# First mixer layer's r projection as seven block products placed behind q and k, in a two-layer GLA / chunked-attention trunk

## Chip, core and metric

The kernel runs on one core of one Trainium2 chip. The metric is device time in microseconds (us) of one execution; lower is better. Everything is float32 to the outside. TensorE works on fp32r operands, and each float32 operand is split into a high and a low part, so that one product of two float32 tiles is three matmuls (hi x hi, hi x lo, lo x hi).

## What is computed

Two layers on 512 tokens of width 1024. Layer 0 is gated linear attention (GLA), then a SwiGLU feed-forward; layer 1 is chunked softmax attention, then a feed-forward; each is followed by a layer norm with a residual. The change lies in the GLA mixer alone:

```python
q, k, v, r, g_low = split(x @ w_in, [512, 1024, 2048, 3072])    # x: 512 x 1024
log_a = log_sigmoid(g_low @ w_gate_up + b_gate) / 16
cum = cumsum(log_a)                       # within chunks
q_dec = q * exp(cum);  k_inv = k * exp(-cum);  k_end = k * exp(total - cum)
a = causal(q_dec @ k_inv^T);  o = a @ v + q_dec @ state
state = state * exp(total) + k_end^T @ v
y = silu(r) * layernorm(o) * norm_g
out = y @ w_out
```

r is x (512 x 1024) times a 1024 x 1024 weight. It is used only in the last step, as the gate of the normalised o.

## The kernel before

The program is written by hand for five engines, each with its own instruction list; semaphores order them. Weights come as "slabs" of 128 x 1024 floats, two to a DMA of 1 MB (a pair), issued by SP into one of two raw buffers (`raw`, slot = pair number modulo 2; the feed-forward's down projection has two more). A raw slot is free when both slabs of its pair are split. ACT copies a slab to `w_hi` (`split_hi`, line 638), then POOL (line 1179) or VectorE (DVE, line 1330) subtracts to get `w_lo`. `w_hi` and `w_lo` are rings of four slabs: `split_hi(n)` waits until TensorE (PE) is done with slab n-4 (`slab_done`), and PE waits for the low part (`lo_done`) of the slab it begins. ACT, DVE, POOL and SP each work in program order, so a wait holds everything behind it on that engine.

The GLA stage has the slabs in this order: v (8), r (8), q and k (8, alternating by head), then the output projection (8, `GLA_OUT`). PE's order:

- `token_major(0, GLA_V, ...)`: v, 24 matmuls of 128x512 to a slab. Each of the two halves of v's columns fills four PSUM banks, which ACT copies out (line 893).
- 16 matmuls for the gate's low-rank input (lines 2283, 2284), then r by `token_major(1, GLA_R, ...)`, 24 matmuls to a slab, with four matmuls of the gate (`gate_up`) after r's first slab. ACT applies Silu straight from the banks (line 932) and POOL multiplies by `norm_g` (line 1255).
- q and k, 24 matmuls to a slab. In the meantime DVE runs the cumulative sums (line 1795) and ACT the exponentials (lines 915 to 920), and DVE scales q and k out of the banks (lines 1814 to 1821).
- The recurrence over four tiles of 128 tokens: `turn_ke` (transposes of k_end, line 2317), `gla_scores` (line 2324), `updates` (line 2331), `intra` (line 2338), `inter` (line 2346), `turn_y` (line 2140). Around it ACT copies o out (`copy_o`) and normalises it (`normalise_o`, line 951), DVE masks scores (line 1833), updates the state (lines 1847, 1849), takes the statistics (`stats_o`, lines 1872, 1875), the shift (line 1882) and the gate product (`gate_o`, line 1859), and POOL takes the root (lines 1263, 1264) between the two.
- The output projection of GLA, the feed-forward, and so on.

The feed-forward's down projection already works by seven half-size block products (the Winograd form of Strassen's scheme). Its sums of weight blocks are made in DRAM by DMAs that POOL issues (`block_sum`, lines 1207 and 1209; every second one adds into its destination), each waiting for the one before. The tables that it uses are the ones that the change uses too:

```python
INTO = ("x", "z", "y", "x", "y", "x", "w")
SOURCES = (("down", 0), ("down", 2), ("sums", 0), ("sums", 1), ("down", 3), ("sums", 2), ("sums", 3))
SUM_STEPS = ((0, "down", 0), (0, "down", 1), (1, "sums", 0), (1, "down", 3),
             (2, "down", 1), (2, "down", 3), (3, "sums", 1), (3, "down", 2))
SUM_READY = {2: 2, 3: 4, 5: 6, 6: 8}
```

`SUM_READY` says how many of the eight DMAs must have landed before product p's weights may be loaded. In the down projection pair q (of 20) takes slot q modulo 4, whatever the parity of the pairs before.

## Time and profile before

| | us |
|---|---|
| median of 3 runs | 1132.55 (1132.28 to 1132.69) |
| the profiled execution, whole | 1132.14 |
| its span in the profile | 1130.40 |
| TensorE busy in the span | 1120.2 (99%) |
| DVE / ACT / POOL busy | 784.6 / 569.8 / 325.6 |

The span is the time from the first to the last instruction in the profile; 1.74 us of the profiled execution lie outside it. Times in the trace count from the span's start. PE's matmuls are pipelined: the interval from one start to the next is its pace, and the shown duration is longer. A weight load overlaps the matmul before it. Idle time of an engine other than the one that sets the end costs nothing by itself.

### The profile page before, as it was taken

Reading aid. Unit: us, or ns where it says so; the run is one execution under the profiler, and the core shown is the slowest. Engines: PE = TensorE matmul, PEld = TensorE weight load, DVE = VectorE, ACT = ScalarE, POOL = GpSimd, SP = SyncE. Lnnn points to the kernel's source line nnn. Section 1 sums busy time; section 2 is a strip of 40 time slices with the busy share of each in tenths; the row PEclk is TensorE's granted clock in tenths of the full one; section 3 lists DMA queues with packets and bytes.
Section 4 is the critical chain, followed back from the end, with each engine's and each line's share of the span. In section 5 each row is a group of like instructions: output and inputs, shape, how many; then the busy total and the mean of one; then the engine's idle time right before and its main releaser. Section 6 shows DMA issues by size and latency. Waiting matters only on the chain.

```text
span 1130.4 us, 18412 instructions
## 1 busy us (share of the span) xinstructions
PE 1120.2 (99%) x6828; PEld 994.7 (88%) x6828; DVE 784.6 (69%) x1263; ACT 569.8 (50%) x926; POOL 325.6 (29%) x215
## 2 busy tenths in 40 slices
PE   9999999999999999999999999999999999999997
PEld 7888888989999999888887787778989999998886
DVE  5070163798888885998604676766878888868987
ACT  4345144244555556555515565772445555556553
POOL 1538525142222112000445343551412222230001
PEclk9999999999999999999999999999999999999999
DMA  6433314076897764654332212132159879827551
GB/s 227 167 150 112 112 38 149 13 271 164 273 279 211 245 182 175 234 197 170 108 112 75 95 47 94 48 150 75 38 191 279 237 248 280 214 74 298 189 193 75
DMA packets 34459, 183.35 MB, mean 162 GB/s; under 512 B 3152, under 2 KB 7376, under 8 KB 20704
## 3 DMA queue, kind: packets, MB, share of 16 engines
q1 hardware_dynamic: 19472, 122.27, 30.1%
q0 software_dynamic: 8448, 46.14, 15.8%
...
## 4 chain that ended last, share of the span: by engine, by line
PE 96%; DVE 1%; issue 1%; DMA 1%; ACT 0%; POOL 0%; SPq 0%; DVEq 0%; POOLq 0%; ACTq 0%
PE bank L2057 29%; PE bank L2059 29%; PE bank L2058 29%; PE bank L2509 2%; PE bank L2493 2%; PE bank L2140 1%; PE bank L2088 1%; PE bank L2530 1%; PE bank L2529 1%; DMA s_raw<-stream 1%; PE bank L2338 1%; DVE s_w_lo L1330 1%; PE bank L2331 0%; PE bank L2346 0%; PE bank L2324 0%
## 5 line engine op out<-in xcount | busy, mean ns | idle before, releaser
L2057 PE MATMUL bank<-s_t_hi,s_w_hi 128*128 128x256 f32 (+1 forms) x832 | 264.4, 318 | 0.0
L2058 PE MATMUL bank<-s_t_lo,s_w_hi 128*128 128x256 f32 (+1 forms) x832 | 262.8, 316 | 0.0
L2059 PE MATMUL bank<-s_t_hi,s_w_lo 128*128 128x256 f32 (+1 forms) x832 | 262.8, 316 | 0.0
L1179 POOL TENSOR_TENSOR s_w_lo<-s_raw,s_w_hi 128x1024 fp32r<-128x1024 f32 x64 | 160.1, 2512 | 180.3 <-ACT s_w_hi L638 180.3
L638 ACT ACTIVATE s_w_hi<-s_raw 128x1024 fp32r<-128x1024 f32 x107 | 111.3, 1057 | 114.6 <-PE bank L2059 90.5
L2059 PEld LDWEIGHTS bank<-s_t_hi,s_w_lo 128*128 128x128 f32 x832 | 158.6, 191 | 10.2
L2057 PEld LDWEIGHTS bank<-s_t_hi,s_w_hi 128*128 128x128 f32 x832 | 158.7, 191 | 9.7 <-issue 0.2
L2058 PEld LDWEIGHTS bank<-s_t_lo,s_w_hi 128*128 128x128 f32 x832 | 158.7, 191 | 9.4
L1216 POOL TENSOR_TENSOR s_w_lo<-s_raw,s_w_hi 128x512 fp32r<-128x512 f32 x36 | 67.2, 1866 | 274.3 <-ACT s_w_hi L768 274.3
L2057 PE MATMUL bank<-s_t_hi,s_w_s_hi 128*128 128x256 f32 x432 | 122.4, 283 | 0.0
L2059 PE MATMUL bank<-s_t_hi,s_w_s_lo 128*128 128x256 f32 x432 | 122.2, 283 | 0.0
L2058 PE MATMUL bank<-s_t_lo,s_w_s_hi 128*128 128x256 f32 x432 | 122.2, 283 | 0.0
L2057 PE MATMUL bank<-s_w_hi,s_t_hi 128*128 128x512 f32 x264 | 104.2, 395 | 0.0
L2059 PE MATMUL bank<-s_w_hi,s_t_lo 128*128 128x512 f32 x264 | 102.9, 390 | 0.0
L2058 PE MATMUL bank<-s_w_lo,s_t_hi 128*128 128x512 f32 x264 | 102.8, 389 | 0.0
L2057 PEld LDWEIGHTS bank<-s_t_hi,s_w_s_hi 128*128 128x128 f32 x432 | 82.9, 192 | 0.1
L2058 PEld LDWEIGHTS bank<-s_t_lo,s_w_s_hi 128*128 128x128 f32 x432 | 82.9, 192 | 0.0
L2059 PEld LDWEIGHTS bank<-s_t_hi,s_w_s_lo 128*128 128x128 f32 x432 | 82.9, 192 | 0.0
L1187 POOL TENSOR_SCALAR s_var_eps<-s_variance 128x1 f32<-128x1 f32 x15 | 4.9, 324 | 244.5 <-ACT s_squared L672 244.5
L1330 DVE TENSOR_TENSOR s_w_lo<-s_raw,s_w_hi 128x1024 fp32r<-128x1024 f32 x40 | 48.9, 1222 | 28.5 <-ACT s_w_hi L638 14.1
L2059 PEld LDWEIGHTS bank<-s_w_hi,s_t_lo 128*128 128x128 f32 x264 | 49.6, 188 | 10.5
L2057 PEld LDWEIGHTS bank<-s_w_hi,s_t_hi 128*128 128x128 f32 x264 | 49.6, 188 | 10.1 <-DVE s_t_lo L1336 0.2
...
## 6 DMA issues: line engine op xcount, KB each, us to landing
s_raw<-stream SPq DMA_DIRECT2D x75, 1024.0 KB, 4.8
sums<-down POOLq DMA_DIRECT2D x12, 2816.0 KB, 20.9
s_more_raw<-sums SPq DMA_DIRECT2D x12, 1024.0 KB, 4.9
sums<-sums POOLq DMA_DIRECT2D x4, 2816.0 KB, 12.9
s_raw<-down SPq DMA_DIRECT2D x8, 1024.0 KB, 4.9
s_ln_gb<-ln_gb ACTq DMA_DIRECT2D x4, 1024.0 KB, 7.0
s_more_raw<-down SPq DMA_DIRECT2D x4, 1024.0 KB, 7.5
s_raw<-sums SPq DMA_DIRECT2D x4, 1024.0 KB, 4.9
```

The source lines that it names most:

```text
L638: nc.scalar.activation(w_parts(n, cols)[0], raw_pair(SLOTS[pair])[:, n % 2, cols], ACT.Copy).then_inc(hi_done, new)
L1179: nc.gpsimd.tensor_tensor(lo, raw_pair(SLOTS[place // 2])[:, n % 2, cols], hi.bitcast(F32), ALU.subtract).then_inc(lo_done, new)
L1216: nc.gpsimd.tensor_tensor(w_lo[:, up_at, HALF:], raw[:, slot, 1, HALF:], w_hi[:, up_at, HALF:].bitcast(F32), ALU.subtract).then_inc(lo_don ...
L1330: nc.vector.tensor_tensor(lo, raw_pair(SLOTS[place // 2])[:, n % 2, cols], hi.bitcast(F32), ALU.subtract).then_inc(lo_done, new)
L2057: nc.tensor.matmul(out, l_hi, r_hi, start=start, stop=False, skip_group_check=skip)
L2058: nc.tensor.matmul(out, l_hi, r_lo, start=False, stop=False, skip_group_check=skip)
L2059: return nc.tensor.matmul(out, l_lo, r_hi, start=False, stop=stop, skip_group_check=skip)
L2088: last = nc.tensor.matmul(bank[bank_of(0, t)][:, :], x, w, start=(k == 0 and low_x + low_w == 0), stop=False)
L2140: last = nc.tensor.transpose(bank[banks[t][half]][:, k * P:(k + 1) * P], src[:, t, (4 * half + k) * P:(4 * half + k + 1) * P], ident[:, :])
L2338: last = nc.tensor.matmul(bank[GLA_O_BANKS[t][hd // 2]][:, (hd % 2) * GLA_DV:(hd % 2 + 1) * GLA_DV], g_am[:, t % 2, hd * P:(hd + 1) * P], ...
L2493: last = nc.tensor.matmul(bank[2 + hd][:, score_columns(t)], qk[q][rows, toks], qk[k][rows, keys], start=(i == 0), stop=(i == 2))
L2509: last = nc.tensor.transpose(bank[4 + hd][:, at:at + P], r_p[:, s % 4, j * P:(j + 1) * P], ident[:, :])
```

## The change

r moves behind q and k, and is computed by seven products of half size instead of eight slabs. A product is 512 x 512 of weights (two slabs of 12 matmuls each) with 256 tokens and 4 blocks of 128 of the inner dimension, so 24 matmuls of 128x512. Four products use sums of weight blocks (`r_sums` in DRAM, made by eight DMAs of POOL of 1 MB each), four use sums of blocks of x (`r_ops`, made by DVE, laid where `h` and `ln_gb` will be loaded, and in one case in `g_rg`). ACT copies the products out of the banks to `g_rg` (`r_copy`), DVE adds the second part (`r_add`), then come Silu and `norm_g` as before, now from SBUF. The loads of `h` and `ln_gb` are issued only after the sixth product. The low parts of the product weights are DVE's for 10 of 14 slabs. The first tile's `turn_ke` and `gla_scores` go ahead of the seventh product. q and k of the first two heads are copied out by ACT (`copy_qk`) and scaled from SBUF. Some semaphores are merged, which changes no order by itself. The core of the diff:

```diff
-GLA_R = GLA_V + KD
-GLA_QK = GLA_R + KD
-GLA_OUT = GLA_QK + 2 * GLA_HEADS
+GLA_QK = GLA_V + KD
+GLA_R = GLA_QK + 2 * GLA_HEADS
+GLA_OUT = GLA_R + 2 * 7
+R_SUM_BYTES = KD // 2 * HALF
...
+        R_BANKS = {"x": (0, 1), "y": (4, 5), "z": (6, 7), "w": (2, 3)}
+        R_QUARTERS = ((0, 0), (1, 0), (0, 1), (1, 1), (2, 1), (3, 1), (2, 0), (3, 0))
...
+                if GLA_R <= n < GLA_OUT:
+                    p = (n - GLA_R) // 2
+                    if p in SUM_READY:
+                        sp.wait_ge(r_blocks, 16 * SUM_READY[p])
+                    array, which = SOURCES[p]
+                    sp.dma_start(raw_pair(slot).rearrange("p a c -> p (a c)"), a["r_" + array][which]).then_inc(raw_full[slot], 16)
+                    continue
...
+            def r_op_highs():
+                for i in range(3):
+                    act.wait_ge(r_op_sum, i + 1)
+                    nc.scalar.activation(r_ops[i]["hi"][:, :, :], r_ops[i]["sum"][:, :, :], ACT.Copy).then_inc(r_op_hi, 1)
...
+            r_split(0, 5)
+            r_done(0)
+            act.wait_ge(qk_scaled, 6)
+            r_copy("x", 0)
+            r_copy("x", 1)
...
+            r_split(11, 14)
+            for n in range(GLA_OUT, GLA_OUT + 2):
+                split_hi(n)
+            r_silu(2)
+            r_silu(3)
+            r_done(5)
+            act.dma_start(h[:, :, :], a["x"].rearrange("(t p) d -> p t d", p=P)).then_inc(h_full, 16)
+            load_gb(0)
+            act.wait_ge(r_op_lo, 4)
+            r_copy("x", 6)
+            r_copy("x", 7)
...
+            ke_tile_out(0)
+            r_silu(4)
+            r_silu(5)
+            split_hi(GLA_OUT + 2)
+            r_silu(6)
+            r_silu(7)
...
+            def r_block_sum(step):
+                to, array, which = SUM_STEPS[step]
+                if step:
+                    pool.wait_ge(r_blocks, 16 * step)
+                if step % 2:
+                    nc.gpsimd.dma_start(a["r_sums"][to], a["r_" + array][which], accum_op=ALU.add,
+                                        max_dma_last_dim=R_SUM_BYTES).then_inc(r_blocks, 16)
+                else:
+                    nc.gpsimd.dma_start(a["r_sums"][to], a["r_" + array][which], max_dma_last_dim=R_SUM_BYTES).then_inc(r_blocks, 16)
+
             for n in range(GLA_V, GLA_R):
                 split_lo(n + RING)
+                if n % 2 == 1:
+                    r_block_sum(n // 2)
...
+            scale_r(0)
+            scale_r(1)
+            pool.wait_ge(lo_done, GLA_OUT)
+            scale_r(2)
+            scale_r(3)
+            split_lo(GLA_OUT)
+            for quarter in range(4, 8):
+                scale_r(quarter)
+            split_lo(GLA_OUT + 1)
+            root_o(0)
+            split_lo(GLA_OUT + 2)
+            root_o(1)
...
+            r1, r2, r4 = (r_ops[i]["sum"][:, :, :] for i in range(3))
+            nc.vector.tensor_tensor(r1, x_half(0, LATE_TOKS), x_half(1, LATE_TOKS), ALU.subtract).then_inc(r_op_sum, 1)
+            dve.wait_ge(r_op_sum, 1)
+            nc.vector.tensor_tensor(r2, r1, x_half(0, EARLY_TOKS), ALU.subtract).then_inc(r_op_sum, 1)
...
+            dve.wait_ge(lo_done, GLA_R + RING)
+            r_low(4, 7)
+            dve.wait_ge(slab_done, GLA_R + 4)
+            dve.wait_ge(r_copied, 2)
+            r_add(0, None, "z", ALU.add)
+            r_add(1, None, "z", ALU.add)
+            r_low(7, 10)
+            dve.wait_ge(r_op_hi, 4)
+            r_op_low(0, g_rg[:, 2:4, 0:HALF].rearrange("p t (k c) -> p t k c", k=2))
+            r_low(10, 14)
+            dve.wait_ge(slab_done, GLA_R + 10)
+            dve.wait_ge(r_copied, 6)
+            r_add(2, "y", None, ALU.subtract)
+            r_add(3, "y", None, ALU.subtract)
...
-            token_major(1, GLA_R, lambda half, t: 4 - 4 * half + t, r_free, beside=gate_up)
...
+            for p in range(PRODUCTS):
+                if p == 0:
+                    pe.wait_ge(abs_done, GLA_HEADS)
+                    pe.wait_ge(min_done, GLA_HEADS)
+                if p == 1:
+                    pe.wait_ge(qk_scaled, 3 * GLA_HEADS)
+                if 2 <= p <= 5:
+                    pe.wait_ge(r_op_lo, p - 1)
+                if 3 <= p <= 5:
+                    pe.wait_ge(r_copied, 2 * (p - 2))
+                if p == PRODUCTS - 1:
+                    pe.wait_ge(consts, 7)
+                    pe.wait_ge(r_merged, 4)
+                    turn_ke(0)
+                    gla_scores(0)
+                op_hi_, op_lo_ = r_operand(p)
+                for j in range(KD // 2):
+                    n = GLA_R + 2 * p + j // 2
+                    if j % 2 == 0:
+                        pe.wait_ge(lo_done, place_of(n) + 1)
+                    for i in range(2):
+                        toks = slice(i * P, (i + 1) * P)
+                        last = three(bank[R_BANKS[INTO[p]][i]][:, :], op_hi_[:, j, toks], op_lo_[:, j, toks],
+                                     *w_parts(n, slice(j % 2 * HALF, (j % 2 + 1) * HALF)),
+                                     INTO[p] not in INTO[:p] and j == 0, j == KD // 2 - 1, True)
+                    if j % 2:
+                        last.then_inc(slab_done, 1)
```

On POOL the stretch from the first weight split to the recurrence's first two roots stands so before (`s_w_lo` is a slab's low part, `s_g_rg` is r times `norm_g`, `s_var_eps_o` and `s_rstd_o` are the root):

```order
L1179 TENSOR_TENSOR s_w_lo<-s_raw,s_w_hi 128x1024 x12
L1255 TENSOR_TENSOR s_g_rg<-s_g_rg,s_norm_g 128x512 x2
L1179 TENSOR_TENSOR s_w_lo<-s_raw,s_w_hi 128x1024
L1255 TENSOR_TENSOR s_g_rg<-s_g_rg,s_norm_g 128x512 x2
L1179 TENSOR_TENSOR s_w_lo<-s_raw,s_w_hi 128x1024 x3
L1255 TENSOR_TENSOR s_g_rg<-s_g_rg,s_norm_g 128x512 x4
L1179 TENSOR_TENSOR s_w_lo<-s_raw,s_w_hi 128x1024 x8
L1263 TENSOR_SCALAR s_var_eps_o<-s_mv_o 128x4
L1264 TENSOR_TENSOR s_rstd_o<-s_var_eps_o,s_minus_half 128x4
```

and so of the change, from the seventh of the eight sums on:

```order
L1320 DMA r_sums<-r_sums 512x512
L1247 TENSOR_TENSOR s_w_lo<-s_raw,s_w_hi 128x1024 x2
L1317 DMA r_sums<-r_down 512x512
L1332 TENSOR_TENSOR s_g_rg<-s_g_rg,s_norm_g 128x512 x4
L1247 TENSOR_TENSOR s_w_lo<-s_raw,s_w_hi 128x1024
L1332 TENSOR_TENSOR s_g_rg<-s_g_rg,s_norm_g 128x512 x4
L1247 TENSOR_TENSOR s_w_lo<-s_raw,s_w_hi 128x1024
L1336 TENSOR_SCALAR s_var_eps_o<-s_mv_o 128x4
L1337 TENSOR_TENSOR s_rstd_o<-s_var_eps_o,s_minus_half 128x4
L1247 TENSOR_TENSOR s_w_lo<-s_raw,s_w_hi 128x1024
```

The sums stand between pairs of weight splits, and all eight products by `norm_g` now stand behind the last sum, with two splits of the output projection between them and the first root, and one more split between the first root and the second.

On ACT, around the sixth and seventh product and the recurrence's first turn, the change has this (`s_g_kt` is the copy of the turned k_end, L966 is Silu, L960 the copy of a product out of its bank):

```order
L655 ACTIVATE s_w_hi<-s_raw 128x1024 x5
L966 ACTIVATE s_g_rg<-s_g_rg 128x512 x2
L994 DMA s_h<-x 128x4x1024
L670 DMA s_ln_gb<-ln_gb 128x2048
L960 ACTIVATE s_g_rg<-bank 128x512 x2
L1004 ACTIVATE s_g_kt<-bank 128x512
L966 ACTIVATE s_g_rg<-s_g_rg 128x512 x2
L655 ACTIVATE s_w_hi<-s_raw 128x1024
L966 ACTIVATE s_g_rg<-s_g_rg 128x512 x2
L1004 ACTIVATE s_g_kt<-bank 128x512
```

Before, ACT had this there:

```order
L932 ACTIVATE s_g_rg<-bank 128x512 x4
L638 ACTIVATE s_w_hi<-s_raw 128x1024 x7
L942 ACTIVATE s_g_kt<-bank 128x512
L638 ACTIVATE s_w_hi<-s_raw 128x1024
L942 ACTIVATE s_g_kt<-bank 128x512
```

The copy of the first turned tile, for which PE's `updates(0)` waits, stands behind five weight splits, two Silus, two DMA issues and two bank copies; before, only weight splits stood ahead of it.

## Rows read from the trace of the kernel before

**Rows 1.** The page: busy time of each engine, and the clock granted to TensorE.

```profile
PE 1120.2 (99%) x6828; PEld 994.7 (88%) x6828; DVE 784.6 (69%) x1263; ACT 569.8 (50%) x926; POOL 325.6 (29%) x215
...
PEclk9999999999999999999999999999999999999999
```

**Rows 2.** Waits of PE, longest first: total us, times, longest.

```profile
PE bank L2277 <- DVE s_g_am L1735: 1.4, 1, 1.4
PE bank L2509 <- DVE s_pt_lo L1953: 0.8, 2, 0.5
PE bank L2088 <- ACT s_w_hi L876: 0.3, 1, 0.3
```

**Rows 3.** Timeline of PE, v: start, us, what (first and last of 120).

```profile
23.01 0.39 PE L2057 MATMUL bank<-s_w_hi,s_t_hi 128*128 128x512 f32 x1
...
49.98 0.39 PE L2059 MATMUL bank<-s_w_hi,s_t_lo 128*128 128x512 f32 x1
50.21 0.39 PE L2283 MATMUL bank<-s_t_hi,s_wg 128*128 128x512 f32 x1
```

**Rows 4.** Timeline of PE, the recurrence.

```profile
141.79 0.60 PE L2317 MATMUL bank<-s_ident,s_g_ke 128*128 128x128 f32 x4
142.22 1.06 PE L2324 MATMUL bank<-s_g_q,s_g_ki 128*128 128x128 f32 x8
143.16 1.97 PE L2331 MATMUL bank<-s_g_v,s_g_kt 128*128 128x256 f32 x8
...
160.61 1.04 PE L2140 MATMUL bank<-s_ident,s_g_on 128*128 128x128 f32 x8
```

**Rows 5.** The page's DMA issues: KB of each, median us to landing.

```profile
s_raw<-stream SPq DMA_DIRECT2D x75, 1024.0 KB, 4.8
sums<-down POOLq DMA_DIRECT2D x12, 2816.0 KB, 20.9
...
sums<-sums POOLq DMA_DIRECT2D x4, 2816.0 KB, 12.9
...
bias_rows<-rel_bias ACTq DMA_DIRECT2D x1, 3072.0 KB, 12.3
```

**Rows 6.** Timeline of POOL: four sum DMAs of the down projection.

```profile
242.87 0.90 POOL L1209 DMA_DIRECT2D sums<-down  x1
...
268.16 1.07 POOL L1207 DMA_DIRECT2D sums<-down  x1
...
290.54 0.67 POOL L1209 DMA_DIRECT2D sums<-sums  x1 [4.11 <-DMA sums<-down]
...
307.83 1.02 POOL L1207 DMA_DIRECT2D sums<-down  x1 [1.24 <-DMA sums<-sums]
```

**Rows 7.** Timeline of DVE while POOL splits weights, with one add just before.

```profile
230.04 0.69 DVE L1588 TENSOR_TENSOR s_t_sum<-s_t_sum,s_t_lo 128x512 f32<-128x512 f32 x1
...
231.37 2.60 DVE L1588 TENSOR_TENSOR s_t_sum<-s_t_sum,s_t_lo 128x512 f32<-128x512 f32 x1
```

**Rows 8.** Timeline of POOL, splits: beside those DVE adds, and in v.

```profile
231.01 2.41 POOL L1179 TENSOR_TENSOR s_w_lo<-s_raw,s_w_hi 128x1024 fp32r<-128x1024 f32 x1 [13.87 <-ACT s_w_hi L638]
...
25.46 9.52 POOL L1179 TENSOR_TENSOR s_w_lo<-s_raw,s_w_hi 128x1024 fp32r<-128x1024 f32 x4 [22.19 <-ACT s_w_hi L638]
```

**Rows 9.** Timeline of ACT: splits of slabs, copies of banks, Silu.

```profile
24.24 3.19 ACT L638 ACTIVATE s_w_hi<-s_raw 128x1024 fp32r<-128x1024 f32 x3
...
90.52 2.07 ACT L932 ACTIVATE s_g_rg<-bank 128x512 f32<-128x512 f32 x4
```

**Rows 10.** Timeline of DVE: a slab's low part, the first statistics, last mask.

```profile
19.26 1.22 DVE L1751 TENSOR_TENSOR s_w_lo<-s_raw,s_w_hi 128x1024 fp32r<-128x1024 f32 x1
...
149.34 1.41 DVE L1872 BATCH_NORM_STATS2 s_bn_o<-s_g_on 128x6 f32<-128x256 f32 x4 [2.12 <-ACT s_g_on L961]
...
159.65 0.73 DVE L1833 COPY_PREDICATED s_g_am<-s_causal,bank 128x512 f32<-128x512 int32 x1
```

**Rows 11.** Timeline of POOL: products by norm_g, and the first root.

```profile
91.64 2.55 POOL L1255 TENSOR_TENSOR s_g_rg<-s_g_rg,s_norm_g 128x512 f32<-128x512 f32 x2
...
151.25 0.24 POOL L1263 TENSOR_SCALAR s_var_eps_o<-s_mv_o 128x4 f32<-128x4 f32 x1 [4.85 <-DVE s_mv_o L1875]
```

**Rows 12.** Timeline of SP: first loads of the down projection, loads behind it.

```profile
417.55 10.47 SPq L600 DMA_DIRECT2D s_raw<-down  x2
...
529.16 5.12 SPq L592 DMA_DIRECT2D s_raw<-stream  x2
```

**Rows 13.** Timelines: ACT's splits of those loads, and DVE behind the last.

```profile
433.92 1.05 ACT L638 ACTIVATE s_w_hi<-s_raw 128x1024 fp32r<-128x1024 f32 x1
...
537.46 1.99 ACT L638 ACTIVATE s_early<-s_raw 128x1024 fp32r<-128x1024 f32 x2
...
543.13 1.28 DVE L1336 TENSOR_TENSOR s_t_lo<-bank,s_t_hi 128x512 fp32r<-128x512 f32 x2
```

More of the change, by code:

```diff
@@ L180, in build_program @@
         t_lo = sb("t_lo", [P, KD, SEQ], F32R)
+        h_at = place[0]
         h = sb("h", [P, TILES, D_MODEL])
@@ L312, in build_program @@
         wg_raw = get("wg_raw", [P, KD, GLA_RANK])
+        qk_raw = sb_at("qk_raw", [P, 2, 2, SEQ], F32, rg_at)
+        r_ops = [halves_at(f"r_op{i}", [P, KD // 2, SEQ // 2], at_, at_ + 4 * KB)
+                 for i, at_ in enumerate((h_at, h_at + 8 * KB, gb_at))]
         get, _ = carve(on_at, region_end)
@@ L653, in load_gb, with token_major @@
                 act.dma_start(ln_gb[:, :, :], a["ln_gb"][n].partition_broadcast(P)).then_inc(gb_full, 16)
-            def token_major(which, n0, bank_of, copy_out):
+            def token_major(which, n0, bank_of, copy_out, between=None):
                 for half in range(2):
+                    if half == 1 and between is not None:
+                        between()
                     for k in range(KD // 2):
@@ L911, in _, with copy_qk @@
             nc.scalar.activation(g_e[:, :, :], g_e[:, :, :], ACT.Ln, bias=1.0).then_inc(log_done, 1)
-            for n in range(GLA_R, GLA_R + EARLY_R):
+            def copy_qk(hd, is_k):
+                act.wait_ge(slab_done, GLA_QK + 2 * hd + is_k + 1)
+                nc.scalar.activation(qk_raw[:, hd, is_k, :], bank[4 + 2 * hd + is_k][:, :], ACT.Copy).then_inc(qk_copied, 1)
+            for n in range(GLA_QK, GLA_QK + EARLY_QK):
                 split_hi(n + RING)
-            act.wait_ge(centred_cum, 1)
+            for hd in range(2):
+                for is_k in range(2):
+                    copy_qk(hd, is_k)
@@ L935, in _, with r_split, r_done, r_copy @@
-            for n in range(GLA_QK, GLA_OUT - 1):
-                split_hi(n + RING)
+            def r_split(first, end):
+                for slab in range(first, end):
+                    split_hi(GLA_R + slab)
+            def r_done(p):
+                act.wait_ge(slab_done, GLA_R + 2 * p + 2)
+            def r_copy(b, quarter):
+                t, half = R_QUARTERS[quarter]
+                nc.scalar.activation(g_rg[:, t, half * HALF:(half + 1) * HALF], bank[R_BANKS[b][t % 2]][:, :],
+                                     ACT.Copy).then_inc(r_copied, 1)
@@ new lines, in r_silu @@
+            def r_silu(quarter):
+                t, half = R_QUARTERS[quarter]
+                act.wait_ge(r_merged, quarter + 1)
+                nc.scalar.activation(g_rg[:, t, half * HALF:(half + 1) * HALF], g_rg[:, t, half * HALF:(half + 1) * HALF],
+                                     ACT.Silu).then_inc(tok_out[1], 1)
+            r_split(0, 5)
[3 more added lines that the diff above has]
+            r_copy("x", 1)
+            r_split(5, 8)
@@ new lines, in _ @@
+            r_silu(0)
+            r_silu(1)
+            r_split(8, 9)
+            r_done(2)
+            act.wait_ge(r_op_sum, 4)
+            nc.scalar.activation(r_ops[0]["hi"][:, :, :], g_rg[:, 2:4, 0:HALF].rearrange("p t (k c) -> p t k c", k=2),
+                                 ACT.Copy).then_inc(r_op_hi, 1)
+            r_copy("y", 4)
+            r_copy("y", 5)
+            r_split(9, 11)
+            r_done(3)
+            r_copy("x", 2)
+            r_copy("x", 3)
+            r_split(11, 14)
@@ new lines, in r_low, with r_add @@
+            def r_low(first, end):
+                for slab in range(first, end):
+                    split_low(GLA_R + slab)
+            def r_add(quarter, first, second, op):
+                t, half = R_QUARTERS[quarter]
+                out = g_rg[:, t, half * HALF:(half + 1) * HALF]
+                first, second = (out if b is None else bank[R_BANKS[b][t % 2]][:, :] for b in (first, second))
+                nc.vector.tensor_tensor(out, first, second, op).then_inc(r_merged, 1)
+            dve.wait_ge(lo_done, GLA_R + RING)
@@ L1834, in mask_scores @@
                                           bank[4][:, :]).then_inc(sc_masked, 1)
+            dve.wait_ge(am_zeroed, 3)
+            dve.wait_ge(consts, 7)
+            mask_scores(0)
+            dve.wait_ge(slab_done, GLA_R + 14)
+            r_add(6, None, "w", ALU.add)
+            r_add(7, None, "w", ALU.add)
             def update_state(t):
@@ L2353, in turn_y @@
                 turn(GLA_YT, t, g_on, GLA_Y_BANKS)
-            pe.wait_ge(consts, 7)
             pe.wait_ge(tok_out[0], 2 * TILES)
-            pe.wait_ge(qk_scaled, 3 * GLA_HEADS - 1)
-            turn_ke(0)
-            gla_scores(0, range(GLA_HEADS - 1))
-            pe.wait_ge(qk_scaled, 3 * GLA_HEADS)
-            gla_scores(0, (GLA_HEADS - 1,))
-            pe.wait_ge(tok_out[1], 2 * TILES)
             for t in range(TILES):
@@ L2376, in _ @@
                 pe.wait_ge(sc_masked, t + 1)
+                if t == 0:
+                    pe.wait_ge(r_merged, 2 * TILES)
                 if t >= 2:
```

176 lines of the change are left out of this document (91 added, 85 removed).

## The prediction

> **What bounds the kernel now.** I read the page first. TensorE (PE) is busy for 99% of the span and its clock stands at the full level (2.4 GHz) in all 40 slices [rows 1]. A busy PE alone proves little, since its durations overlap, so I went to PE's waits: over the whole run they add up to some 3 us, and the longest after the start is 0.5 us [rows 2]. In the stretch that the change touches, 6 to 190 us, PE waits for nobody after v's first slabs. So time falls by the matmuls taken from PE, less the waits that the new order makes. The third view is PE's timeline. Through v, 120 matmuls of 128x512 start from 23.01 to 50.21 us, where the next line begins [rows 3]: 27.20 / 120 = 0.2267 us each. The recurrence runs at the same kind of pace from 141.79 us on, with nothing between its lines [rows 4].
>
> **Removed from PE.** r was 8 slabs of 24 such matmuls, 192, or 43.5 us. It becomes 7 products of 24, 168, or 38.1 us, of the same shape. 24 x 0.2267 = **5.44 us** less. Nothing is added on PE: `turn_ke(0)` and `gla_scores(0)`, 1.37 us from 141.79 to 143.16 [rows 4], only stand ahead of the seventh product. What is left is whether everybody can keep up. I walked the new order by hand from 25 to 160 us, each instruction at the interval that the rows show for its kind and each wait at the later of its two sides. New times below are from this walk: q starts at 53.8, the products at 98.3, the recurrence's `updates(0)` at 137.7, and the output projection is reached 5.4 to 5.7 us earlier than before.
>
> **The weight sums.** Eight DMAs of 1 MB by POOL, each waiting for the one before, stand between POOL's splits from 31 us on, so a late sum holds the splits behind it. Before has no DMA of 1 MB of this kind. The nearest are the down projection's, of 2.75 times the bytes: 20.9 us, or 12.9 for the copy of a sum [rows 5]. One by one, the copy issued at 242.87 and the add at 268.16 show what POOL's next issue waits for: it goes out at 290.54, some 22 us behind the add, and the copy of 290.54 has landed by 307.83 [rows 6]. By bytes alone a copy of 1 MB is 12.9 / 2.75 = 4.7 and an add 20.9 / 2.75 = 7.6 us; that is the lower bound. The upper one is no gain from size, 13 and 21 us, because both kinds have 512 rows (here of 2 KB instead of 5.5). The bias copy, 3 MB in rows of 1.5 KB, lands in 12.3 us [rows 5], so short rows alone do not make a copy slow. I take 6 and 9 us, near the lower end with a little for a fixed part. In the walk the last sum, behind the split of slab 19, is issued at 102 and lands at 111, and the load that needs it goes out at 119. Nothing waits up to 9 and 12 us, beyond 0.3. At 9 and 13 PE loses 1.3 us, at 10 and 14 it loses 7.7, at 13 and 21 some 46.
>
> **POOL and DVE together.** A DVE add of 128x512 with all operands in SBUF took 0.69 us just before POOL's split, and 2.60 us when it began 0.36 us into that split [rows 7, 8]: POOL's 2.41 us end at 233.42, and 0.6 later the add ends. One waits for the other. The change puts three adds and three low parts of x between POOL's splits of slabs 4 to 7, which ran without a gap before, 9.52 us for four [rows 8]. Taking turns, slab 7's low part comes at 43.1 us instead of 35, and PE wants it at 44.8. It holds, with 1.6 us left. The same turns can push the low part of the gate's rank-16 input behind a split: in the walk it ends 0.4 us before `gate_up` at 59.3, and in the worst phase it is late by 1.2. I take 0 to 1.2, near 0.2.
>
> **Splits and loads for the products.** A slab now lasts PE 12 x 0.2267 = 2.72 us. With a ring of four, three slabs (8.2 us) lie between a freed place and the need for it. ACT's split takes 1.0 us and a bank copy 0.5 [rows 9], DVE's low part 1.2 [rows 10]. A pair's load, 4.8 us [rows 5], has six slabs (16.3 us) less both splits. With the bank copies, adds and Silus in between, the least margin of the walk is 3.2 us, ahead of the fifth product. `turn_ke(0)` wants the adds of quarters 2 and 3, with 1.7 us left, and `updates(0)` wants `ke_tile_out(0)`, which ACT has behind its splits and the two DMA issues, with 2.0 left. `intra(0)` wants the last two adds, with 1.5 left. These edits cost nothing while these margins last; each us beyond them is a us on PE.
>
> **POOL before the first root.** The eight products by `norm_g`, 1.27 us each (2.55 for two) [rows 11], now end in a row of six with two splits that begins at 132.7 us, when ACT has done Silu 2, and ends at 145.0. The first root is wanted when the statistics are done, at 145.6 (before, 9.5 us behind `turn_ke(0)`: 151.25 [rows 11]). It is free 0.7 us early. What queues behind the root is the shift, the second mask, `gate_o(0)`, the second statistics, and in the end the last mask, for which `turn_y(0)` waits. Before, that mask was done at 160.38 [rows 10] and `turn_y(0)` began at 160.61 [rows 4], so that chain has only some 0.3 us to give. If the statistics (149.34, 1.41 us, one input in SBUF [rows 10]) wait for POOL's last split as the adds in rows 7 do, it all moves by 1.2 us and PE loses 0.8; if not, 0. I take 0, for only the adds with two inputs have been seen waiting.
>
> The Trainium skill, SBUF — State Buffer, section "Who interferes with whom", has this as a lock that VectorE takes with two SBUF inputs and that it and GpSimd hold for a whole instruction. By that rule the statistics, with one input, go free and the sum keeps its 5.44 us; read from the add's row alone without telling the inputs apart, it would be 4.7.
>
> **The parity of pairs.** r has 6 slabs more, so every later pair has the other raw slot, but the down projection begins at slot 0 all the same. Its first load then follows directly on the pair that is freed last: its two first loads went out at 417.55 and by 427.69 us [rows 12] (10.47 in all, with 0.33 for the issue), and now both go at the second time. The split of the first came at 433.92 [rows 13]; 427.7 + 4.8 = 432.5, in time by 1.4 us, in both layers. Behind layer 0's down projection the load of 529.16 likewise moves to the time of the next, 534.0 (529.16 + 5.12 less the issue) [rows 12], and lands near 538.8, where ACT's split stood at 537.46 [rows 13]: 1.3 us late on ACT, ahead of the transposed tiles, for which DVE had its step only at 543.13 [rows 13]. I take 0, and up to 1.3 as the bound.
>
> **Sum.** 1130.40 - 5.44 + 0.3 for small waits = 1125.3 us of span; with 1.74 us outside it 1127.0. The profiled execution was 0.41 us under the median of the runs, so **1127.4 us**.
>
> **The rivals.** A difference under 0.2% (2.3 us) is about what a measurement here cannot tell from none.
> - The case above, with 0 to 1.2 us of waits: 1127.1 to 1128.3. For it speaks that each margin came out positive. Chance 0.65.
> - The recurrence's first turn is late, as POOL reaches the root behind its eight products (a split beside DVE's work has taken more than 2.4 us). Each us past 0.7 at the root is nearly one on PE. With 2 us: 1129.1. Against it: DVE reads PSUM in most of that stretch. 0.10.
> - The sums land late. This is the one that can end slower: from 10 and 14 us for copy and add the 5.4 us are gone (1134.8 with 7.7 lost), and every further us per pair costs more. At 9 and 13: 1128.4. Against it stands the bias copy's row. For it stand equal row counts and loads beside them. 0.14, of it 0.03 faster, 0.05 same, 0.06 slower.
> - The other raw slot holds up a transition: 1 to 3 us, so 1129.1. 0.07, of it 0.02 same.
> - The change does not do what it says: the products' matmuls run slower than v's, as they change operands between `t_hi`, `r_ops` and two token tiles, or a wait that I did not see. v too changes its stationary tile at each three matmuls and keeps 0.2267. 1132 to 1136. 0.04.
>
> **How the numbers follow.** Faster by over 0.2% (under 1130.3): 0.65 + 0.07 of the second case (the rest of it, 0.03, falls within 0.2%) + 0.03 + 0.05 = 0.80. Same: 0.03 + 0.05 + 0.02 + 0.02 = 0.12. Slower: 0.06 + 0.02 = 0.08. The range begins at 1126.7, for 5.44 us and the 0.3 us by which the recurrence could start with less of a gap, and reaches to 1131.5, which leaves some 0.12 above. The likeliest case alone has 1126.7 to 1128.3.
>
> **What would show it.** Right: PE without a wait over 0.5 us between 50 and 165 us; the products from about 98.3 to 137.7; the output projection 5.4 us earlier; the sum DMAs landing in 5 to 10 us, the last by 112. Wrong: PE waiting for `s_w_lo` in the second product (late sums), for `s_g_am` or `s_g_rg` in the recurrence (late root or adds), for `s_low_rows` near 59 (turns of POOL and DVE), or for `s_w_lo` at 436 or 1013 (parity).

## The result, and the profile after

| | before | changed |
|---|---|---|
| median of 9 runs each, us | 1132.38 (1131.97 to 1132.69) | 1135.66 (1133.33 to 1137.72) |
| the profiled execution, whole / span | 1132.14 / 1130.40 | 1133.33 / 1131.3 |
| mean granted clock | 0.999 in the profiled execution, 0.998 to 0.999 in the later batches | 0.993 to 0.999 over the nine runs |

The changed kernel is slower by 3.3 us: ratio 1.0029, 95% interval 1.0019 to 1.0039. The prediction, 1127.4 us in a range of 1126.7 to 1131.5, is missed, and on the other side of no change. The profiled execution is the fastest of the nine: its span is only 0.9 us longer than before's. So the profile shows a part of the loss, and the median has more.

The page of the changed kernel, answering to [rows 1]:

```profile
PE 1115.3 (99%) x6804; PEld 990.2 (88%) x6804; DVE 840.9 (74%) x1290; ACT 587.7 (52%) x948; POOL 326.1 (29%) x219
```

PE has 24 matmuls and 4.9 us of busy time less, and the products run at v's pace: from the start of the third at 111.39 us, 66 matmuls take 14.96 us, 0.2267 each. PE's waits in the changed kernel, total us, times, longest, beside [rows 2]:

```profile
PE bank L2288 <- DVE s_g_am L1978: 3.8, 1, 3.8
PE bank L2205 <- DVE s_g_ki L1936: 2.5, 1, 2.5
PE bank L2425 <- DVE s_g_am L1824: 1.4, 1, 1.4
PE bank L2682 <- DVE s_pt_lo L2101: 0.8, 2, 0.5
```

The two upper waits are new. L2205 is the first matmul of the second product, which waits for q and k to be scaled; L2288 is `turn_y(0)`, which waits for the last mask. 1130.4 - 5.44 + 2.49 + 3.77 = 1131.2, which is the profiled span of 1131.3. So in this execution these terms account for the whole span.

**The first wait.** DVE in the changed kernel, the scalings of heads 0 and 1, and then the first that reads a bank; below it POOL in the same stretch:

```profile
89.93 0.69 DVE L1930 SCALAR_TENSOR_TENSOR s_g_q<-s_qk_raw,s_g_q 128x512 f32<-128x512 f32 x1 [3.05 <-ACT s_g_ke L949]
90.53 0.55 DVE L1934 TENSOR_TENSOR s_g_ke<-s_qk_raw,s_g_ke 128x384 f32<-128x384 f32 x1
91.00 2.90 DVE L1936 TENSOR_TENSOR s_g_ki<-s_qk_raw,s_g_ki 128x512 f32<-128x512 f32 x1
93.83 2.88 DVE L1930 SCALAR_TENSOR_TENSOR s_g_q<-s_qk_raw,s_g_q 128x512 f32<-128x512 f32 x1
96.63 3.00 DVE L1934 TENSOR_TENSOR s_g_ke<-s_qk_raw,s_g_ke 128x384 f32<-128x384 f32 x1
99.55 2.88 DVE L1936 TENSOR_TENSOR s_g_ki<-s_qk_raw,s_g_ki 128x512 f32<-128x512 f32 x1
102.36 0.68 DVE L1930 SCALAR_TENSOR_TENSOR s_g_q<-bank,s_g_q 128x512 f32<-128x512 f32 x1
```

```profile
90.92 5.23 POOL L1247 TENSOR_TENSOR s_w_lo<-s_raw,s_w_hi 128x1024 fp32r<-128x1024 f32 x2 [6.54 <-ACT s_w_hi L655]
...
96.78 5.11 POOL L1247 TENSOR_TENSOR s_w_lo<-s_raw,s_w_hi 128x1024 fp32r<-128x1024 f32 x2
```

Before POOL's first split an operation takes 0.55 to 0.69 us; beside the four splits it takes 2.9 to 3.0, so the two alternate, one DVE operation to one split. Four times some 2.3 us of extra time put the end of the last scaling at 105.76, and PE starts at 105.81. The same line, L1930, is fast again at 102.36, when the splits have ended and it reads a bank (`a` below tells these two apart).

The chain ahead of the scalings was late as well. The four cumulative sums (line 1908) took 13.13 us beside four splits, where they had taken 10.97 beside three (line 1795). The exponentials and the first scaling stand behind them. Up to 2.2 of the 2.5 us may therefore be their share; no run takes it apart.

**The second wait.** DVE behind the two roots, and POOL there:

```profile
146.08 1.41 DVE L2021 BATCH_NORM_STATS2 s_bn_o<-s_g_on 128x6 f32<-128x256 f32 x4 [2.10 <-ACT s_g_on L1030]
...
149.47 2.23 DVE L2031 SCALAR_TENSOR_TENSOR s_shift_o<-s_mv_o,s_rstd_o 128x4 f32<-128x4 f32 x1
151.63 0.73 DVE L1978 COPY_PREDICATED s_g_am<-s_causal,bank 128x512 f32<-128x512 int32 x1
...
158.37 2.21 DVE L2031 SCALAR_TENSOR_TENSOR s_shift_o<-s_mv_o,s_rstd_o 128x4 f32<-128x4 f32 x1
160.51 0.71 DVE L1978 COPY_PREDICATED s_g_am<-s_causal,bank 128x512 f32<-128x512 int32 x1
```

```profile
144.94 2.35 POOL L1247 TENSOR_TENSOR s_w_lo<-s_raw,s_w_hi 128x1024 fp32r<-128x1024 f32 x1
...
147.99 0.23 POOL L1336 TENSOR_SCALAR s_var_eps_o<-s_mv_o 128x4 f32<-128x4 f32 x1 [0.70 <-DVE s_mv_o L2024]
148.31 1.05 POOL L1337 TENSOR_TENSOR s_rstd_o<-s_var_eps_o,s_minus_half 128x4 f32<-128x4 f32 x1
149.34 2.34 POOL L1247 TENSOR_TENSOR s_w_lo<-s_raw,s_w_hi 128x1024 fp32r<-128x1024 f32 x1
```

The shift has 4 elements to a partition, and takes 2.2 us, because POOL began a split 0.13 us ahead of it. POOL was in time at the root (it sat idle for 0.70 us before it). The statistics at 146.08, with one input in SBUF, began within the split of 144.94 and took 1.41 us, as before. The shift, twice, delays the mask behind it, and the second one ends PE's wait.

The Trainium skill, SBUF — State Buffer, section "Who interferes with whom", says this of both places: an instruction of DVE with two SBUF inputs and one of POOL that reads SBUF hold a shared port for their whole length, and the later one blocks. The rows agree in who waits and for how long, down to an instruction of 128x4; the port itself is in no row.

### The profile page after: what moved, and what is told of

It is laid out like the page before. It is cut to its first block, busy times and chain, and to the rows that moved or that the text cites. A ratio compares the mean times of both kernels' runs of the same rounds, so it can differ in the third digit from the quotient of the medians.

```text
span 1131.3 us, 18450 instructions
## 1 busy us (share of the span) xinstructions
PE 1115.3 (99%) x6804; PEld 990.2 (88%) x6804; DVE 840.9 (74%) x1290; ACT 587.7 (52%) x948; POOL 326.1 (29%) x219
## 4 chain that ended last, share of the span: by engine, by line
PE 91%; DVE 4%; issue 2%; ACT 1%; DMA 1%; POOL 0%; DVEq 0%; POOLq 0%; SPq 0%; ACTq 0%
PE bank L2205 27%; PE bank L2207 27%; PE bank L2206 27%; PE bank L2682 2%; PE bank L2666 2%; PE bank L2236 1%; PE bank L2288 1%; DVE s_w_lo L1419 1%; PE bank L2703 1%; PE bank L2702 1%; DMA s_more_raw<-down 1%; DVE s_g_ki L1936 1%; DVE s_g_q L1930 0%; PE bank L2425 0%; DVE s_g_ke L1934 0%
## 5 line engine op out<-in xcount | busy, mean ns | idle before, releaser
L2205 PE MATMUL bank<-s_t_hi,s_w_hi 128*128 128x256 f32 (+1 forms) x832 | 264.4, 318 | 0.0
L1247 POOL TENSOR_TENSOR s_w_lo<-s_raw,s_w_hi 128x1024 fp32r<-128x1024 f32 x60 | 154.0, 2587 | 146.2 <-ACT s_w_hi L655 146.1
L655 ACT ACTIVATE s_w_hi<-s_raw 128x1024 fp32r<-128x1024 f32 x113 | 117.6, 1058 | 96.3 <-PE bank L2207 79.0
L2205 PEld LDWEIGHTS bank<-s_t_hi,s_w_hi 128*128 128x128 f32 x832 | 158.7, 191 | 9.7 <-issue 0.2
L2205 PE MATMUL bank<-s_t_hi,s_w_s_hi 128*128 128x256 f32 x432 | 122.4, 283 | 0.0
L2205 PE MATMUL bank<-s_w_hi,s_t_hi 128*128 128x512 f32 x224 | 89.0, 397 | 2.5 <-DVE s_g_ki L1936 2.5
L1419 DVE TENSOR_TENSOR s_w_lo<-s_raw,s_w_hi 128x1024 fp32r<-128x1024 f32 x50 | 61.7, 1234 | 37.8 <-ACT s_w_hi L655 23.3
L2207 PE MATMUL bank<-s_w_hi,s_t_lo 128*128 128x512 f32 x224 | 87.4, 390 | 0.0
L2206 PE MATMUL bank<-s_w_lo,s_t_hi 128*128 128x512 f32 x224 | 87.2, 389 | 0.0
L2205 PEld LDWEIGHTS bank<-s_t_hi,s_w_s_hi 128*128 128x128 f32 x432 | 82.9, 192 | 0.1
L823 ACT ACTIVATE s_prod<-bank 128x256 f32<-128x256 f32 x36 | 13.9, 385 | 85.9 <-PE bank L2207 85.9
L655 ACT ACTIVATE s_w_hi<-s_more_raw 128x1024 fp32r<-128x1024 f32 (+1 forms) x38 | 38.6, 1034 | 32.7 <-PE bank L2207 28.5
```

The lines of the kernel that those rows point to most:

```text
L655: nc.scalar.activation(w_parts(n, cols)[0], raw_pair(SLOTS[pair])[:, n % 2, cols], ACT.Copy).then_inc(hi_done, new)
L823: nc.scalar.activation(parts_of(j)[3], bank[banks["a"][j]][:, EARLY_TOKS], ACT.Silu).then_inc(gated[f], 1)
L1247: nc.gpsimd.tensor_tensor(lo, raw_pair(SLOTS[place // 2])[:, n % 2, cols], hi.bitcast(F32), ALU.subtract).then_inc(lo_done, new)
L1419: nc.vector.tensor_tensor(lo, raw_pair(SLOTS[place // 2])[:, n % 2, cols], hi.bitcast(F32), ALU.subtract).then_inc(lo_done, new)
L2205: nc.tensor.matmul(out, l_hi, r_hi, start=start, stop=False, skip_group_check=skip)
L2206: nc.tensor.matmul(out, l_hi, r_lo, start=False, stop=False, skip_group_check=skip)
```

## The experiments

Ten kernels follow; `d` and `i` leave out a factor of the shift, `e` the sums. "The mask wait" below is PE's wait ahead of `turn_y(0)`, 3.8 us in the changed kernel. Times are medians; before stood at 1132.17 to 1132.32 in the same batches.

| label | median us (runs) | ratio, 95% | profiled span |
|---|---|---|---|
| a_wait_scaled | 1133.66 (11) | 1.0014 (1.0004 to 1.0023) | 1130.8 |
| b_wait_shift | 1131.03 (11) | 0.9987 (0.9978 to 0.9996) | 1129.3 |
| ab_both_waits | 1127.60 (5) | 0.9963 (0.9949 to 0.9977) | 1125.6 |
| c_before_splits_behind_roots | 1137.64 (5) | 1.0048 (1.0034 to 1.0062) | 1135.7 |
| d_one_input_shift | 1134.01 (10) | 1.0014 (1.0004 to 1.0023) | 1132.9 |
| e_no_sums | 1126.70 (4) | 0.9951 (0.9936 to 0.9966) | 1124.7 |
| f_adds_ahead | 1126.83 (5) | 0.9955 (0.9941 to 0.9968) | 1125.1 |
| g_before_one_split | 1134.21 (10) | 1.0018 (1.0008 to 1.0027) | 1131.9 |
| i_reduce_shift | 1127.80 (6) | 0.9964 (0.9951 to 0.9976) | 1125.7 |
| j_filled_wait | 1136.67 (5) | 1.0038 (1.0024 to 1.0052) | 1134.9 |

### The first wait alone

```diff
             for n in range(GLA_V, GLA_R):
+                if n + RING == GLA_R:
+                    pool.wait_ge(qk_scaled, 6)
                 split_lo(n + RING)
```

> Edit: in the changed kernel POOL waits for the six scalings of heads 0 and 1 before it splits the products' first slab. Theory (POOL and DVE take turns on SBUF: each all-SBUF scaling waits for one POOL split): those scalings take 0.55 to 0.7 us each, all twelve end near 99.5 us in place of 105.8, and PE's wait of 2.49 us ahead of the second product is gone; the wait of 3.8 us ahead of turn_y(0) stays. Span 1128.5 to 1129.2 where the clock is 0.999, median of runs 1129.5 to 1133, since one stall of PE is left that may still bring lower granted clocks. Rival (the scalings are late because their inputs, the exponentials, are late): exps are 1.6 us later than before, so the wait ahead of the second product stays above 1.5 us and the time is unchanged at about 1135. Rival (the late weight sums matter): POOL's delayed splits put the last two sums 3 us later, and PE then waits for a low part in the products, no gain.

The first wait is gone from PE's list and the second stands, 3.7 us. So the holds of the scalings caused it, and neither rival (late exponentials alone, late sums) stands. The scalings that read a bank are not held, though they too run beside splits (0.55 to 0.68 us each, here one of them):

```profile
94.22 0.55 DVE L1936 TENSOR_TENSOR s_g_ke<-bank,s_g_ke 128x384 f32<-128x384 f32 x1
```

```profile
93.79 4.76 POOL L1247 TENSOR_TENSOR s_w_lo<-s_raw,s_w_hi 128x1024 fp32r<-128x1024 f32 x2 [10.19 <-DVE s_g_ki L1938]
```

But the span, expected at 1128.5 to 1129.2 for a clock of 0.999, is 1130.8, no run has that clock (0.995 to 0.997; spans 1130.6 to 1133.0), and the median of 1133.66 lies 0.7 above its range. The profile of this run shows a part of the reason. PE behind `turn_y(0)`'s wait, and the granted clock of stretches there (columns: stretch, its length, PE's busy time and instructions, clock, DMA share, GB/s):

```profile
159.43 1.12 PE L2290 MATMUL bank<-s_ident,s_g_on 128*128 128x128 f32 x8 [3.75 <-DVE s_g_am L1980]
160.36 3.58 PE L2518 MATMUL bank<-s_g_v,s_g_am 128*128 128x256 f32 x8
...
165.32 0.58 PE L2207 MATMUL bank<-s_w_hi,s_t_hi 128*128 128x512 f32 x1
```

```profile
160.00:161.00 1.00, 1.00 (x7) 0.68 0.55 164
161.00:162.00 1.00, 1.00 (x3) 0.50 0.99 418
162.00:163.00 1.00, 1.00 (x4) 0.50 0.91 385
163.00:164.00 1.00, 1.00 (x5) 0.61 0.01 0
164.00:165.00 1.00, 1.00 (x6) 1.00 0.00 0
```

The clock falls to the level of 1.2 GHz just behind the wait; the missing shares of these rows add up to 1.7 us. The eight matmuls of `intra(3)` take 3.58 us, and 1.89 at 2.4 GHz. From `turn_y(0)` to the output projection it is 165.32 - 159.43 = 5.89 us, and 165.47 - 161.28 = 4.19 in the profiled execution of the change, where the clock stayed up after a wait as long. So this stall cost its own length and 1.7 us more, and the span is accounted for: 1130.4 - 5.44 + 3.75 + 1.7 + 0.4 (a wait ahead of `turn_ke(0)`) = 1130.8. The slower of the eleven runs, up to 1133.0, have up to 2.2 us more that no profile shows.

### The second wait alone

```diff
             root_o(0)
+            pool.wait_ge(shift_done, 1)
             split_lo(GLA_OUT + 2)
             root_o(1)
+            pool.wait_ge(shift_done, 2)
             split_lo(GLA_OUT + 3)
```

> Edit: in the changed kernel POOL waits for the first shift before it splits GLA_OUT+2, and for the second before GLA_OUT+3. Theory (the 128x4 shift of DVE with two SBUF inputs waits for the whole split that POOL begins just before it): both shifts take 0.16 us, PE's wait of 3.77 us ahead of turn_y(0) is gone or under 0.3; the wait of 2.5 us ahead of the second product stays. Span 1127.4 to 1128.0 at a clock of 0.999; median of runs 1128.5 to 1132. Rival (the recurrence is late because POOL reaches the root late, behind its eight products by norm_g): the wait stays above 2 us, time about 1135.

The mask wait is gone and the first one stays at 2.5 us; the kernel is now slightly faster than before. Its eleven runs fall into two groups: three with spans of 1127.7 to 1127.9 at a clock of 0.999, and eight with 1129.1 to 1130.0 at 0.996 to 0.998. The profile is of the second group. PE behind the wait of 2.48 us, and the clock there:

```profile
106.35 0.80 PE L2207 MATMUL bank<-s_w_hi,s_t_hi 128*128 128x512 f32 x1 [2.48 <-DVE s_g_ki L1938]
...
107.80 0.63 PE L2207 MATMUL bank<-s_w_hi,s_t_hi 128*128 128x512 f32 x1
108.23 0.63 PE L2208 MATMUL bank<-s_w_lo,s_t_hi 128*128 128x512 f32 x1
...
109.99 0.39 PE L2207 MATMUL bank<-s_w_hi,s_t_hi 128*128 128x512 f32 x1
110.22 0.40 PE L2208 MATMUL bank<-s_w_lo,s_t_hi 128*128 128x512 f32 x1
```

```profile
107.00:108.00 1.00, 1.00 (x4) 0.50 0.93 154
108.00:109.00 1.00, 1.00 (x4) 0.50 1.14 209
109.00:110.00 1.00, 1.00 (x5) 0.75 1.11 205
110.00:111.00 1.00, 1.00 (x6) 1.00 1.12 207
```

The pace is 0.43 us to a matmul until about 109.5, and then 0.23 again. The distance of the two groups, 1.6 us between 1127.7 and 1129.3, is what this costs. The median, 1131.03, lies in the range given for it; the range for the span, given for a clock of 0.999, held for the three runs that had that clock.

### Both

> Both edits together. Theory: PE has no wait above 0.5 us between 50 and 165 us; span 1125.0 to 1125.6, whole 1126.8 to 1127.5 in every run, with a granted clock of 0.999 as in the kernel before, if it is PE's stalls that lower the clock in most runs of the changed kernel. Rival for the clock (something else in the change lowers it, as the products' order or the DMAs' load): runs still show 0.993 to 0.997 and the median stands 2 to 3 us above the fastest run.

1127.60 us. DVE's scalings take 0.55 to 0.69 us each and the shift 0.16:

```profile
91.17 0.68 DVE L1940 TENSOR_TENSOR s_g_ki<-s_qk_raw,s_g_ki 128x512 f32<-128x512 f32 x1
...
147.73 0.16 DVE L2035 SCALAR_TENSOR_TENSOR s_shift_o<-s_mv_o,s_rstd_o 128x4 f32<-128x4 f32 x1
```

```profile
...
PE bank L2240 <- ACT s_w_hi L895: 0.7, 1, 0.7
PE bank L2471 <- DVE s_g_rg L1958: 0.7, 1, 0.7
```

The theory's 0.5 us was missed by little: one new wait of 0.7 us is left between 50 and 165 us, ahead of `turn_ke(0)` (L2471; L2240 lies in v's first slabs). POOL's wait for the scalings has a part in it: it moves the last sum's issue from 103.75 to 106.0 us. The clock is 0.998 to 0.999 in every run, as before. The span, 1125.6, is 4.8 us under before's; the expected whole time held in two of five runs, the next two were within 0.15 us, and one had 1129.50, 1.6 us of span above its neighbours at a clock of 0.998, unexplained. The clocks of 0.993 to 0.997 are gone with the two waits, so the rival "something else lowers the clock" falls.

### One part of the change in the kernel before

`c` puts POOL's splits of `GLA_OUT+2` and `+3` behind the first and second root of the kernel before, and changes nothing else; `g` moves only the latter.

```diff
-            for n in range(GLA_QK, GLA_OUT):
+            for n in range(GLA_QK, GLA_OUT - 2):
                 split_lo(n + RING)
             for t in range(TILES):
...
+                if t < 2:
+                    split_lo(GLA_OUT + 2 + t)
```

> Edit in the kernel before: POOL's splits of GLA_OUT+2 and GLA_OUT+3 stand behind the first and the second root, as in the change; nothing else. Theory: the shifts take 2.2 us in place of 0.16, both in one chain, and PE waits 3.6 to 4.1 us ahead of turn_y(0); span 1134.0 to 1134.5 at 0.999, and if a stall of PE there brings lower clocks, a median of 1136 to 1139 with clocks of 0.993 to 0.997. Rival (the stall needs the change's other parts, as the later root): under 1 us, 1132 to 1133.5.

> Edit in the kernel before: only POOL's split of GLA_OUT+3 stands behind the second root. Theory: the second shift alone takes 2.2 us, PE waits 1.7 to 1.9 us ahead of turn_y(0): span 1132.2 to 1132.4 if so short a wait leaves the clock at the full level, 1133.5 to 1134 if the low level follows it as it followed the wait of 3.7 us. Rival (the two late shifts do not add up, the chain has more room): under 1 us.

```profile
PE bank L2142 <- DVE s_g_am L1835: 3.7, 1, 3.7
...
PE bank L2142 <- DVE s_g_am L1835: 1.7, 1, 1.7
```

The mask wait is 3.7 us in `c` (upper row) and 1.7 in `g` (lower row), so this one edit makes the whole second wait, and the two shifts add up. Both theories held. `c` costs 5.3 us of span, of which 3.7 are the wait; a low clock stands behind it here too:

```profile
165.00:166.00 1.00, 1.00 (x7) 0.50 0.43 139
166.00:167.00 1.00, 1.00 (x5) 0.50 1.05 442
```

`g` is the case of a short wait. Its clock stays at 1.00 (stretch 162 to 164 us, directly behind the wait), its mean is 0.998 to 0.999 in all ten runs, and the spans are 1131.9 to 1133.0, around the range given for the full clock.

```profile
162.00:164.00 2.00, 1.86 (x13) 1.00 0.70 193
```

### Does idleness lower the clock?

In `c`, ahead of PE's wait for the last mask:

```diff
+                    pe.wait_ge(ke_out, TILES - 1)
+                    for _ in range(16):
+                        nc.tensor.matmul(bank[5][:, :], t_hi[:, 0, 0:P], t_hi[:, 0, :], start=True, stop=True)
                     pe.wait_ge(sc_masked, TILES)
```

> Base: the kernel before with both splits behind the roots (1137.6 us). Edit: PE runs 16 matmuls of 128x512 on a bank that is free (their result is not used) ahead of its wait for the last mask, 3.6 us of work in a wait of 3.7. Theory (the low clock behind the wait comes from PE's idleness, and costs about 1.6 us): intra(3) and inter(3) run at the full level, 1.89 us each, clock 0.998 to 0.999 in every run, 1135.8 to 1136.3. Rival (the clock falls for another reason, as the program's place or the DMAs then running): as before, 1137.6; or, if the 16 take longer than the wait, up to 0.2 us more.

```profile
160.56 4.03 PE L2378 MATMUL bank<-s_t_hi 128*128 128x512 f32 x16
164.73 1.09 PE L2142 MATMUL bank<-s_ident,s_g_on 128*128 128x128 f32 x8
165.66 1.89 PE L2340 MATMUL bank<-s_g_v,s_g_am 128*128 128x256 f32 x8
```

`turn_y(0)` starts at 164.73, against 164.57 in `c`, and yet the kernel is 1.0 us faster. `intra(3)` runs at 1.89 us (2.46 in `c`), and the clock is 0.998 to 0.999 in all five runs. `c` and `j` differ only in the lines shown, so the low level behind the wait comes from PE's idleness. The median of 1136.67 is 0.4 above the range given. The size was expected at 1.6; from `turn_y(0)` to the output projection it is 5.59 us in `c` and 4.20 here, so 1.4, of which 0.2 went to the later start.

### Which operations wait for POOL?

Base of both is `a_wait_scaled`, where the splits stand right behind the roots. Only the shift is changed: in `d` to a multiplication of the mean by -1, in `i` to a reduction over an axis of length one. Both have one SBUF input, and both leave out the factor of the root (`i` the sign too).

```diff
-                nc.vector.scalar_tensor_tensor(out=shift_o[:, t, :], in0=mv_o[:, t, :, 0], scalar=-1.0,
-                                               in1=rstd_o[:, t, :], op0=ALU.mult, op1=ALU.mult).then_inc(shift_done, 1)
+                nc.vector.tensor_scalar(shift_o[:, t, :], mv_o[:, t, :, 0], -1.0, None, ALU.mult).then_inc(shift_done, 1)
```

> Base: the changed kernel with POOL's wait for the scalings. Edit: the shift reads one SBUF operand (minus the mean; the factor of the root is left out, so the normalised o is wrong), POOL's splits stay right behind the roots. Theory (only an operation of DVE with two SBUF inputs waits for POOL): the 128x4 operation takes under 0.2 us although POOL's split runs beside it, and PE's wait ahead of turn_y(0) is under 0.3 us; 1127.6 us as with both waits. Rival (any all-SBUF operation of DVE waits for POOL's split): it takes 2.2 us and the run stays near 1133.7.

> Base: the changed kernel with POOL's wait for the scalings (1133.7 us). Edit: the shift is a reduction of one SBUF operand over an axis of length one (it copies the mean; sign and root's factor are left out, so the normalised o is wrong); POOL's splits stay right behind the roots. The one-input multiplication by a constant still took 2.25 us there. Theory 2 (any operation of DVE that reads SBUF only, and begins within a split, waits): 2.2 us again and 1133 to 1134.5; the statistics at 146.08 in the changed kernel, 1.41 us beside a split, speak against it.

DVE in `d`, and then POOL and DVE in `i`:

```profile
149.62 2.25 DVE L2033 TENSOR_SCALAR s_shift_o<-s_mv_o 128x4 f32<-128x4 f32 x1
```

```profile
147.94 2.36 POOL L1247 TENSOR_TENSOR s_w_lo<-s_raw,s_w_hi 128x1024 fp32r<-128x1024 f32 x1
...
148.06 0.16 DVE L2033 TENSOR_REDUCE s_shift_o<-s_mv_o 128x4 f32<-128x4 f32 x1
```

My theory for `d` fell: with one input the multiplication waits just as long, 2.25 us, and the kernel stays at 1134.01. So the number of inputs is not the whole rule. The reduction, at the same place with the split begun 0.12 us ahead (147.94), takes 0.16 us, and the mask wait is gone: 1127.80 us, as with POOL's wait. The same section of the Trainium skill, SBUF — State Buffer, "Who interferes with whom", lists this too: a `tensor_scalar` can run in a mode that uses both of DVE's port pairs and then contends, a reduction never does. The runs agree on both, with one multiplication and one reduction tried; I had read it for the number of inputs alone. Two runs of `i` stood at 1128.6 and 1129.2, unexplained.

### The sums, and the last wait

`e` leaves out the eight sum DMAs, and loads unsummed blocks of the same size in their place. `f` moves one step on DVE:

```diff
-            r_low(10, 14)
+            r_low(10, 13)
             dve.wait_ge(slab_done, GLA_R + 10)
             dve.wait_ge(r_copied, 6)
             r_add(2, "y", None, ALU.subtract)
             r_add(3, "y", None, ALU.subtract)
+            r_low(13, 14)
```

> Base: the changed kernel with both waits of POOL (1127.6 us). Edit: the eight sum DMAs are left out and the products that use sums load an unsummed block of the same size, so r is wrong. Theory (the sums, 6 to 12 us each, are hidden): 1126.8 to 1127.6, PE's busy time and all waits as they were but for the 0.7 us ahead of turn_ke(0), whose adds stand behind splits of slabs that were loaded late; that one may go. Rival (16 MB of DRAM traffic and late loads cost time on PE elsewhere): below 1126.5.

> Base: the changed kernel with both waits of POOL (1127.6 us). Edit: DVE's adds of quarters 2 and 3 stand ahead of the low part of r's last slab instead of behind it. Theory: PE's last new wait, 0.7 us ahead of turn_ke(0), goes; 1126.8 to 1127.1 us. Rival: the wait has another releaser (the mask's constants or the bank) or the last slab's low part is late in its place: 1127.4 to 1128.

Without the sums the median is 1126.70 us (0.1 under the range given), and the wait of 0.7 at `turn_ke(0)` is gone; with the adds ahead and all sums in place 1126.83, and it is gone too. So with both waits of POOL in place the sums cost those 0.7 us and next to nothing else, and `f` gets them back. In the changed kernel the four copies landed in 6.2 to 8.4 us and the four adds in 8.4 to 11.8:

```profile
r_sums<-r_down POOLq DMA_DIRECT2D x6, 1024.0 KB, 8.9
...
r_sums<-r_sums POOLq DMA_DIRECT2D x2, 1024.0 KB, 6.8
```

They are not free of risk. In `d`'s profile the load of the fifth product's weights, issued at 108.09 beside the last sum, landed after 10.2 us (the median of these loads is 5.0), was split by ACT only at 118.31, and PE waited 1.4 us for the bank copies behind that split:

```profile
118.31 1.06 ACT L655 ACTIVATE s_w_hi<-s_raw 128x1024 fp32r<-128x1024 f32 x1 [4.10 <-DMA s_raw<-r_down]
```

`f_adds_ahead` is the best version that computes all of r: 5.3 us of span under before, for 5.44 removed.

## Why the prediction was wrong, point by point

- **Removed from PE: right.** 24 matmuls at the old pace. With every new wait gone the span is 1125.1 (`f`), and the sum said 1125.3.
- **The weight sums: nearly right.** 6 us for a copy and 9 for an add were taken; 6.2 to 8.4 and 8.4 to 11.8 were measured, and the last sum landed at 113.7 instead of 111. PE waited for none in the changed kernel. The margin of 1.7 us at `turn_ke(0)` was not enough in `ab`, where the last sum goes out 2.2 us later still.
- **POOL and DVE together: the step that failed.** The prediction found the turns in v and was right that PE would not wait there (slab 7's low part came at 37.2 us, not at 43.1; the gate's low part 1.1 us in time). It then did not ask the same question at the places behind v. "Splits and loads for the products" gave DVE's and ACT's margins, and had no price for q and k being scaled from SBUF; it named 3.2 us as the least margin among the products. Four scalings wait for a split each, about 9 us in all, and the second product waits 2.5. The cumulative sums ahead of them are 2.2 us longer, which the walk did not have either. [Rows 7] already had the price of a held operation.
- **POOL before the first root: the second failure.** It saw the chain that has only 0.3 us to give, and priced the root's lateness and the statistics. Both cost nothing. The list of POOL's order shown with the change has a split right behind the first root, and the diff one behind the second; each starts 0.13 or 0.14 us before the shift, which is DVE's next instruction, and neither was asked about. Together they cost 3.8 us. `c` shows that it needs nothing else from the change. The section closed with "only the adds with two inputs have been seen waiting", and the shift, with two inputs though no add, was not counted among them. (The 4.7 us that the passage names for held statistics should be 5.44 - 0.8 = 4.6.)
- **The clock: a term that was missing.** No step said what a stall of PE costs beyond its length. In the profiles of `a`, `b` and `c` it is 1.4 to 1.7 us for one wait, and the mean clocks of the other runs fit the same; `j` shows that idleness is the cause. Of the changed kernel no execution with the low clock was profiled. Its nine runs go from 1131.3 us at 0.999 to 1135.9 at 0.993, and two such stretches (3.2 us) leave up to 1.4 us open. The mean clock says the same: one stretch as in `a` takes 1.7 of 1130 us, or 0.0015, and a fall from 0.999 to 0.993 is four times that. The end of the kernel is at the low level in every profile, where it costs nothing (1.3 us off the mean in the change's profile, 2.6 in `d`'s), and can explain about one of the four. So the slowest three runs had more time at the low level than the two waits are known to bring. Where, stays open.
- **The parity of pairs: right, it cost nothing.** No wait of PE at either down projection, though the first loads took a median of 6.3 us in place of 4.9.
- **The rivals.** "The first turn is late" had the right place, and the wrong cause and size: POOL's lateness, at one us for each. The fifth, at a chance of 0.04, had the right size, 1132 to 1136, as "a wait that I did not see", without saying which.

The sum as it should have stood: 1130.40 - 5.44 + 2.5 + 3.8 = 1131.3 of span, and with one to two stretches at the low clock 1132.9 to 1134.5, so 1134.6 to 1136.2 for the whole. The median was 1135.66. The two waits in it are measured; how many low stretches the median run had is not.
